# The expert loop of a hybrid decoder step: TensorE's products ordered by array width

## What is computed

```
def run_block(args):                       # one block of rows of one expert
    e, toks, g = args
    xb = xpad[toks]                        # gather tokens
    hb = jax.nn.silu(xb @ w1_e[e]) * (xb @ w3_e[e])     # 1024 -> 256, twice
    return (hb @ w2_e[e]) * g[:, None]     # 256 -> 1024, times the gate
out = zeros.at[slot_tok].add(yb)           # scatter and add
```

## Time and profile before

| what | value |
|---|---|
| time, median of 3 runs | 1148.14 us (1147.12 to 1151.25) |
| span of the profiled execution, first to last instruction | 1144.5 us |
| around the span, if that execution ran as those | 2.6 to 6.8 us |
| TensorE (PE) busy | 1087.3 us, 95% of the span |
| VectorE (DVE) busy | 495.5 us, 43% |
| ScalarE (ACT) busy | 288.6 us, 25% |
| GpSimd (POOL) busy | 243.9 us, 21% |
| moved by DMA | 319.77 MB, mean 279 GB/s |

### The profile page before, as it was taken

How to read it: one execution, slowest core, us unless ns; L and a number is a source line. 1 busy time by engine, 2 the same in 40 slices (tenths; PEclk the granted TensorE clock), 3 DMA queues, 4 the chain that set the end, 5 groups by cost and what they waited for, 6 DMA issues and landing times.

```text
span 1144.5 us, 22216 instructions
## 1 busy us (share of the span) xinstructions
PE 1087.3 (95%) x8721; PEld 718.2 (63%) x8721; DVE 495.5 (43%) x1429; ACT 288.6 (25%) x615; POOL 243.9 (21%) x300
## 2 busy tenths in 40 slices
PE   7999998999997989989999999999999999999996
PEld 6888665877883857847555555555556555565531
DVE  0349999224028444681323333233343333423236
ACT  1112163004033041411223222222222322222220
POOL 3120040000000001031333323333333333343300
PEclk9999999999999999998999999999999999999998
DMA  9630315016034853175999999999999999999696
GB/s 331 271 147 1 147 32 183 2 60 251 3 119 148 323 200 133 56 288 217 394 404 409 412 411 415 408 410 414 410 417 410 403 421 407 409 416 387 256 387 262
DMA packets 67122, 319.77 MB, mean 279 GB/s; under 512 B 11069, under 2 KB 17429, under 8 KB 40397
## 3 DMA queue, kind: packets, MB, share of 16 engines
q1 hardware_dynamic: 51269, 278.60, 61.2%
q0 software_dynamic: 14336, 35.48, 8.2%
q10 hardware_dynamic: 1424, 4.35, 1.0%
HBM read 299.36 MB, written 28.58 MB: 287 GB/s over the span
## 4 chain that ended last, share of the span: by engine, by line
PE 73%; DVE 17%; DMA 5%; ACT 2%; issue 2%; SPq 0%; POOL 0%; DVEq 0%; ACTq 0%; POOLq 0%
PE psum L846 65%; PE psum L861 8%; DVE act_mem L1884 7%; DVE mk_mem L2049 2%; DMA arena<-y_rows 2%; DMA mk_mem<-x_rows,idx_x 2%; DMA arena<-in_w_in_dram 2%; DVE act_mem L2105 0%; ACT act_mem L1649 0%; DVE act_mem L2256 0%; DVE act_mem L1984 0%; ACT act_mem L1658 0%; DVE act_mem L2268 0%; DVE act_mem L1982 0%; DVE act_mem L1952 0%
## 5 line engine op out<-in xcount | busy, mean ns | idle before, releaser
L846 PE MATMUL psum<-arena,act_mem 128*32 128x128 f32 (+6 forms) x5488 | 493.4, 365 | 2.1 <-ACT act_mem L1764 1.1
L846 PEld LDWEIGHTS psum<-arena,act_mem 128*32 128x32 f32 (+4 forms) x5488 | 254.4, 120 | 192.6 <-issue 96.7
L846 PE MATMUL psum<-act_mem,arena 128*128 128x260 f32 (+1 forms) x1472 | 328.7, 386 | 8.9 <-DMA arena<-in_w_o_dram 3.8
L846 PEld LDWEIGHTS psum<-act_mem,arena 128*128 128x128 f32 x1472 | 281.0, 196 | 54.1 <-DMA arena<-in_w_o_dram 4.7
L861 PE MATMUL psum<-ident,act_mem 128*128 128x128 f32 (+6 forms) x488 | 79.3, 291 | 15.6 <-DMA act_mem<-in_x_prompt_dram 4.5
L754 POOL DMA_INDIRECT y_rows<-act_mem,idx_y x35 | 39.2, 1120 | 237.4 <-DVE act_mem L2319 214.4
L2317 DVE COPY act_mem<-psum 64x512 f32<-64x512 f32 x35 | 24.3, 693 | 124.7 <-PE psum L846 124.7
L1884 DVE SCALAR_TENSOR_TENSOR act_mem<-act_mem,wcb 128x511 f32<-128x511 f32 (+29 forms) x120 | 77.8, 730 | 0.1
L861 PEld LDWEIGHTS psum<-ident,act_mem 128*128 128x128 f32 (+6 forms) x488 | 57.3, 169 | 29.1 <-issue 17.5
L846 PEld LDWEIGHTS psum<-act_mem 128*96 128x96 bf16 (+5 forms) x419 | 29.9, 123 | 58.2 <-issue 54.6
L2310 DVE SCALAR_TENSOR_TENSOR act_mem<-act_mem,psum 128x128 f32<-128x128 f32 x35 | 12.2, 348 | 114.3 <-ACT act_mem L1720 114.3
(11 more groups left out here) (291 smaller groups left out, 890.8 us busy)
## 6 DMA issues: line engine op xcount, KB each, us to landing
arena<-in_w_e_dram SPq DMA_DIRECT2D x192, 1024.0 KB, 10.2
arena<-y_rows SPq DMA_DIRECT2D x8, 2048.0 KB, 20.4
arena<-in_w_in_dram SPq DMA_DIRECT2D x16, 512.0 KB, 17.7
arena<-in_cache_mem_k_dram SPq DMA_DIRECT2D x8, 1024.0 KB, 8.6
arena<-in_cache_mem_v_dram SPq DMA_DIRECT2D x8, 1024.0 KB, 11.8
arena<-in_w_v_dram SPq DMA_DIRECT2D x1, 4096.0 KB, 24.4
arena<-in_w_k_dram SPq DMA_DIRECT2D x1, 4096.0 KB, 13.9
arena<-in_w_out_dram SPq DMA_DIRECT2D x1, 4096.0 KB, 14.1
```

Of the source, the lines that this page charges most:

```text
L846: return pe.matmul(out, lhsT, rhs, start=first, stop=last)
```

## The change

TensorE's step is put in another order. The up product of a heavy expert and its down product are each cut in two functions, and a step now runs: `up_step(e)` (U64), `down_step(e-1)` (D64), `up_rest(e)` (U32, heavy only), `down_rest(e-1)` (D32, heavy only), `b_step(e+1)` (T8), `a_step(e+3)` (F), `t_step(e)` (T1 or T2, of this step's expert and no longer of the one before). ScalarE's step is rewritten to the same order: silu of e, copies of the down product of e-1, copy of the transposed tokens of e+1, copy of the hidden rows of e. VectorE, GpSimd and SyncE keep their programs. The arithmetic is the same.

```
-            def up_most(b, part):
+            def up_first(b, part):
...
+            def up_more(b, part):
...
-            def down_most(b, part):
+            def down_first(b, part):
...
+            def down_more(b, part):
...
             def step(e, k, i):
 
-                if not is_big(e - 1):
-                    t_step(e - 1, (k - 1) % NB)
-                c_step(e, k % NB, 32 * (NB // 4 * i + (k // 4 + 1)))
+                up_step(e, k % NB, 32 * (NB // 4 * i + (k // 4 + 1)))
+                down_step(e - 1, k - 1, i)
+                up_rest(e, k % NB)
+                down_rest(e - 1, (k - 1) % NB)
                 if exists(e + 1):
                     b_step(e + 1, k + 1, i)
-                y_step(e - 1, k - 1, i)
                 if exists(e + 3):
                     a_step(e + 3, (k + 3) % NB)
+                if exists(e + 1):
+                    t_step(e, k % NB)
...
             def step(e, k, i, sc):
-                if not is_big(e - 1):
-                    h_step(e - 1, (k - 1) % NB)
                 c_step(e, k % NB)
+                y_step(e - 1, k - 1, i, sc)
                 if exists(e + 1):
                     b_step(e + 1, (k + 1) % NB)
-                y_step(e - 1, k - 1, i, sc)
+                    h_step(e, k % NB)
```

More of the change, by code:

```diff
@@ L1303, in up_most @@
                            wu[:, :, k, h:FE:2], k == 0, k == KC - 1)
+            def up_more(b, part):
+                wu, _ = ew(part)
+                both = psum[:, 2, 512 * b:512 * b + 2 * 192].rearrange("p (w n) -> p w n", w=2)
                 for k in range(KC):
@@ L1346, in down_most @@
                            wd[:, k, 512 * h:512 * h + 512], k == 0, k == 1)
+            def down_more(b, part):
+                _, wd = ew(part)
                 for k in range(2):
@@ L1367, in b_step, with up_step @@
                 (turn_rows if is_big(e) else turn_all)(n).then_inc(m_xt, 1)
-            def c_step(e, n, wait_w):
+            def up_step(e, n, wait_w):
                 pe.wait_ge(m_xc, e + 1)
@@ L1373, in c_step, with up_rest, down_step @@
                     pe.wait_ge(m_hd, e - 1)
-                (up_few if is_light(n) else up if is_big(e) else up_most)(n % 2, n % 4).then_inc(m_h, 1)
+                if is_light(n):
+                    up_few(n % 2, n % 4).then_inc(m_h, 1)
+                elif is_big(e):
+                    up(n % 2, n % 4).then_inc(m_h, 1)
+                else:
+                    up_first(n % 2, n % 4)
+            def up_rest(e, n):
+                if not is_light(n) and not is_big(e):
+                    up_more(n % 2, n % 4).then_inc(m_h, 1)
             def t_step(e, n):
-                pe.wait_ge(m_hd, e + 1)
-                (turn_hidden if is_light(n) else turn_hidden_most)(n % 2).then_inc(m_ht, 1)
-            def y_step(e, k, i):
+                if not is_big(e):
+                    pe.wait_ge(m_hd, e + 1)
+                    (turn_hidden if is_light(n) else turn_hidden_most)(n % 2).then_inc(m_ht, 1)
+            def down_step(e, k, i):
                 n = k % NB
@@ L1390, in y_step, with down_rest @@
                     down_few(n % 2, n % 4).then_inc(m_y, 1)
-                else:
-                    (down if is_big(e) else down_most)(n % 2, n % 4).then_inc(m_y, 1)
+                elif is_big(e):
+                    down(n % 2, n % 4).then_inc(m_y, 1)
+                else:
+                    down_first(n % 2, n % 4)
+            def down_rest(e, n):
+                if not is_light(n) and not is_big(e):
+                    down_more(n % 2, n % 4).then_inc(m_y, 1)
             wait_out(pe, "x24")
@@ L1409, in _ @@
             wait_out(pe, "so3")
-            c_step(0, 0, 32)
+            up_step(0, 0, 32)
             b_step(1, 1, 0)
@@ L1446, in _ @@
             t_step(E - 1, NB - 1)
-            y_step(E - 1, NB - 1, LAST)
+            down_step(E - 1, NB - 1, LAST)
+            down_rest(E - 1, NB - 1)
             pe.wait_ge(s_over, 1)
```

## The result

The changed kernel takes 1166.83 us (median of 4 runs, 1165.49 to 1168.44), the kernel before 1147.63 beside it (4 runs, 1146.85 to 1151.25). The ratio is 1.0156, with a 95% interval of 1.0136 to 1.0176: slower, by 19.2 us, where 23.0 were forecast. The span grows by 19.2 too, from 1144.5 to 1163.7.

A forecast was written before the change was run, and what follows sets the result against it. TensorE was taken to set the loop's pace, with DMA just keeping up. Sixty steps at 0.40 us added 24.1 us, less 1.1 at the end: 1148.1 + 23.0 = 1171 us, 2.0% slower, range 1150 to 1180.

The forecast's parts named there:

- What bounds the kernel: Expert loop: TensorE sets the pace, DMA just keeping up; its pieces sum to 143.13 us for sixteen steps.
- Fewer width changes: TensorE's loop steps: fewer changes of array width, 0.07 us per entry or exit; own work 139.35 us in sixteen steps.
- The seams taken at nothing: U64 into D64 and T8 into F, equal width, assumed free; at full price 0.21 us a step is lost.
- The wait for the token copy: Ahead of U64: waits of 1.03 us in light and 0.29 in heavy steps, 11.04 in sixteen steps.
- The size: Whole kernel: net loss of 0.40 us a step, 24.1 in sixty steps, 23.0 after the end's 1.1.
- Faster: Rival: copies don't bind the loop; DMA stops the gain at 1139 us; chance 0.08.
- No change: Rival: waits of 4.61 us in sixteen steps just eat the gain; 1145 to 1152 us; chance 0.07.
- Much slower by the clock: Rival: TensorE's idling in the loop lowers the granted clock to 0.94; 1204 us; chance 0.05.
- What would show it: Loop signs: 35 to 45 us idle ahead of U64, DMA share under 1, experts 8 and 56 451 apart, no gather waits.

The follow-up runs named there:

- experiment 8: Kernel before with half of w2 not loaded from expert 4 on: 1141.73 us, ratio 0.9942.
- experiment 6: Changed kernel with T8, F and the gathers one expert further ahead, and half of w2 not loaded from expert 4 on: 1124.05 us, ratio 0.9798.
- Experiment 1: Changed kernel with ScalarE's old order, its token copy ahead of the down product's copies; TensorE's new order kept: 1152.61 us, ratio 1.0047.
- experiment 3: Changed kernel with up products from expert 2 on reading a fixed SBUF array, so no wait for copied tokens: 1138.27 us, ratio 0.9905.
- experiment 5: Changed kernel with T8, F, indices and gathers one expert further ahead, computation complete: 1137.74 us, ratio 0.9917.
- experiment 4: Changed kernel with T8 ahead of D32 where the down product is heavy, and ScalarE's token copy ahead of the down copies there: 1139.83 us, ratio 0.9932.
- experiment 2: Kernel before with ScalarE's new order alone, TensorE's old order kept: 1243.76 us, ratio 1.0829.
- experiment 7: Changed kernel with half of w2 not loaded from expert 4 on: 1165.94 us, ratio 1.0158.

## Why the prediction was right

**What bounds the kernel** held: TensorE set the pace. The sum of its pieces in the old order was 143.13 for sixteen steps; experiment 8 shows 143.0.

**Fewer width changes.** The seams taken at nothing cost nothing. U64 and D64 take 720.59 - 715.10 = 5.49 us in the changed kernel, where 3.69 + 1.79 = 5.48 were forecast. T8 to F takes 0.99 (forecast 1.02). TensorE's own work is 137.9 by experiment 6, where 139.35 was forecast: the gain is larger by 1.4. I see two reasons in the timelines. F loses its entry too, since T8 has the same width (F to U64 in a light step 0.48 in the earlier trace rows, 0.45 in experiment 6), and F has a shorter form of 128 columns (0.48 in heavy steps), where I took the long one, 0.59, throughout. None of it shortened a step, because the token copy's chain, not TensorE's work, sets U64's start.

**The wait for the token copy** came as forecast in each kind of step. Light: 8.96 us (733.37 - 724.41), forecast 9.02, wait 1.04 for 1.03. Heavy: 9.31 (724.41 - 715.10), forecast 9.35, wait 0.23 for 0.29. With a heavy expert next 9.53 for 9.56; heavy behind heavy 10.58 for 10.69. These are single steps; over the loop light ones take 8.87 to 9.04 and heavy ones behind heavy ones 10.49 to 10.68. Experiment 1 separates its two halves, ScalarE's order and the missing cover. Experiments 3 and 5 take the wait away, experiment 4 most of it (8.7 of 38.8 us are left), and each gets a faster kernel. T2 never waited for VectorE: its product ends at 723.59 and T2 starts at 723.77, behind F, by which it was hidden as forecast.

**The size.** The step that was too large is the net of 0.40 us a step; it measured 0.35 (149.55 - 143.96 = 5.59 in sixteen). Nearly all of the difference is one term: from the end of the token copy to U64 I took 0.11 us, from the one such row behind the loop, and here it is 0.06, or 0.05 behind the heavy step's copy (723.76 + 0.60 to 724.41). 0.05 us in each of sixteen steps is 0.8, and 150.39 - 149.55 is 0.84; in 60 steps that is 3 of the 3.8 us that were missed. The remainder is found at the ends. U64 of the first step and that of expert 62, 61 steps later, before and after:

```profile
527.30 5.82 PE L846 MATMUL psum<-arena,act_mem 128*64 128x256 f32 x96 [0.95 <-issue]
...
1078.48 5.80 PE L846 MATMUL psum<-arena,act_mem 128*64 128x256 f32 x96
```

```profile
527.65 9.43 PE L846 MATMUL psum<-arena,act_mem 128*64 128x256 f32 x104 [0.95 <-issue]
...
1098.09 7.54 PE L846 MATMUL psum<-arena,act_mem 128*64 128x256 f32 x104 [1.11 <-ACT act_mem L1746]
```

The distance grows by 570.44 - 551.18 = 19.3 us, where 61 steps of 0.35 would make 21.3. The 2 us are gather waits. Before, TensorE lost 6.9 us to them in all, but only 3.7 in the 48 steps from which the 0.35 comes. The other 13 steps lost 3.2, where that average would give 1.0, and all of it went away.

Behind the loop two more terms were off, in opposite directions. The first load of results comes 17.46 us later, 2.1 less than U64 and not 1.1, because the wait ahead of U64 lies behind the down product as well. And what lies behind that load did not keep its length: from the load to the end of the span it was 60.3 us and is 62.1. The prediction took the full DMA to set the end. TensorE's rows of the final sum, its start and its last piece, before and after, show that it does so only before:

```profile
1100.13 3.70 PE L846 MATMUL psum<-act_mem 96*128 96x512 f32 x8 [1.28 <-ACT act_mem L1739]
...
1133.28 1.92 PE L846 MATMUL psum<-arena,sum_rows 128*32 128x512 f32 x16 [0.85 <-DMA arena<-y_rows]
```

```profile
1120.37 3.70 PE L846 MATMUL psum<-act_mem 96*128 96x512 f32 x8 [1.28 <-ACT act_mem L1769]
...
1150.75 3.64 PE L846 MATMUL psum<-arena,sum_rows 128*32 128x512 f32 x32
```

Before, the last piece waited for the last load; in the changed kernel TensorE comes to the sum 20.24 us later (0.35 ahead of the first U64, 19.3 from there to expert 62, 0.6 in the last step) and then runs to its end without a wait. The sum gets 1.05 us shorter (1133.28 + 1.92 - 1100.13 = 35.07 before, 1150.75 + 3.64 - 1120.37 = 34.02 after), 0.85 of it by that wait, and 20.24 - 1.05 = 19.2. So the loss arises in the steps of the loop, and the end of the kernel takes 1 us of it back.

**The rivals.** *Faster*: its floor was right and its condition was not met. With the wait gone the kernel ends at 1138 (experiments 3 and 5), where that rival had 1139, by DMA and not by TensorE's work. The prediction set two rules of the Trainium skill against each other (TensorEngine Tiling (Array Packing), Key Properties and PSUM Bottleneck). The first is that a change of tiling mode drains the engine. Experiments 6 and 8 agree with it: the order with fewer changes of mode saves 5.1 us in sixteen steps (137.9 against 143.0). The second is that the copies out of PSUM can become the limit once tiling has made TensorE faster. In the changed kernel a copy does set the pace, but by its place in the order and not by the amount of copies: ScalarE is busy there for 128.69 of 508 us. *No change* had its break-even at waits of 4.61 in sixteen steps. By what was measured the gain is 143.96 - 137.9 = 6.1, larger than forecast, and the waits with it are 149.55 - 137.9 = 11.6, where 11.04 were forecast; so the waits are nearly twice what would have left the time as it was. *Much slower by the clock*: not here, at 1.00. In experiment 2, with waits of up to 2.1 us, the clock did drop, for some 4 us at a time.

**What would show it**: idle time ahead of U64 of 38.8 us (35 to 45 named), experts 8 and 56 448.65 apart (451 named), no gather waits. One sign did not come as named: DMA's share in the loop reads 1.00, not less. It is no measure of spare capacity here: with half of w2 left out the share is 0.90 and the time the same (experiment 7).

## What to carry to other kernels

When work is reordered to save an engine's own time, count what each piece was covering: here T8 had the down product behind it, and setting it ahead of D32 again where that product is heavy, with ScalarE's copies to match, was worth 27 us (1166.8 to 1139.8), more than the 19 that the saved width changes are worth in 60 steps. An in-order engine that is busy for a quarter of the time can still set the pace, if a copy that somebody waits for stands behind one whose input comes last; so put the copy that is needed first ahead and give TensorE work to do meanwhile, or make its input a whole step early. Putting the copy ahead was not enough by itself (experiment 1). And price a wait from both ends of the chain, from the latest input to the first reader, including the row-to-row latency from a place like the one in question.

## What the runs showed of the hardware

- The share of DMA time reads 1.00 to 1.02 at 397, 410 and 415 GB/s (the changed kernel, the kernel before, and experiment 5), and the pace fell behind TensorE's own work in experiments 3 and 5. There the first sixteen steps still ran at TensorE's own 137.9 us; the following ones took 142 to 143, then 140.2. I read this as a lead of weights that had landed early and was used up; that DMA is the cause is shown for experiment 5 by experiment 6.
- In experiment 2 the granted clock was 1.00 from 560 to 706 us, with TensorE busy for 86 to 87 of 100 us and waits of up to 2.1 us. Then it dropped to 0.50 for some 4 us, six times up to 1062 us, each time at the first matmuls behind a wait of 1.7 to 2.0 us, and came back to 1.00 while TensorE was busy. In the changed kernel, busy for 93 of 100 with waits of up to 1.1 us, it stayed at 1.00. Why it fell behind some such waits and not behind others was not tried.
